# Two operand halves in one buffer: a decoder trunk kernel whose conv and gate projections stream 272, 256 and 272 columns instead of 264, 264 and 264

## What is computed

```python
def _mixer(h, S0, buf0, pos, w_in, w_out, ...):
    z = h @ w_in                                    # 2048 -> 7168 columns
    q, k, v, g_r, a, b, g_c = jnp.split(z, SPLITS, axis=-1)   # 7 x 1024
    ...retention over 8 heads from q, k, v, gated by silu(g_r)...
    u = a * jax.nn.sigmoid(b)                       # conv branch input
    full = jnp.concatenate([buf0, u], axis=1)
    c = depthwise_conv(full, w_dw) + b_dw           # width 31
    c = jax.nn.silu(_layer_norm(c, g_cn, b_cn))
    c = c @ w_pw2 + b_pw2
    conv_out = c * jax.nn.silu(g_c)
    m = jnp.concatenate([ret_out, conv_out], axis=-1) @ w_out
```

## Time and profile before

| | |
|---|---|
| median of 3 runs | 1278.45 us (1275.1 to 1279.62) |
| span of the profiled execution | 1272.7 us |
| PE / PEld busy | 1218.1 us (96%) / 1195.9 us |
| DVE busy | 919.9 us (72%) |
| ACT busy | 613.6 us (48%) |
| POOL busy | 136.4 us (11%) |
| chain that ended last | PE 81%, DVE 9%, issue 4%, ACT 3% |

### The profile page before, as it was taken

How to read it: one execution, slowest core, us unless ns; L and a number is a source line. 1 busy time by engine, 2 the same in 40 slices (tenths; PEclk the granted TensorE clock), 3 DMA queues, 4 the chain that set the end, 5 groups by cost and what they waited for, 6 DMA issues and landing times.

```text
span 1272.7 us, 25528 instructions
## 1 busy us (share of the span) xinstructions
PE 1218.1 (96%) x9814; PEld 1195.9 (94%) x9814; DVE 919.9 (72%) x1404; ACT 613.6 (48%) x952; POOL 136.4 (11%) x188
## 2 busy tenths in 40 slices
PE   5999999999999999889998999999999999997998
PEld 5999899999989999789998999999999999996998
DVE  6798898888976532477868879988889764326673
ACT  6342555555546444635544335555554554455341
POOL 0000011112100012401110000211111000123000
PEclk9999999999999999989999999999999999997999
DMA  7555654454543553515554565555544445533462
GB/s 266 189 211 189 191 198 170 180 198 174 211 148 141 202 194 118 182 69 197 198 196 170 199 204 193 182 194 191 192 167 167 154 176 186 182 117 132 152 224 89
DMA packets 42595, 225.71 MB, mean 177 GB/s; under 512 B 6176, under 2 KB 12320, under 8 KB 18976
## 3 DMA queue, kind: packets, MB, share of 16 engines
q1 hardware_dynamic: 28800, 201.47, 44.6%
q10 hardware_dynamic: 13728, 23.33, 5.5%
HBM read 210.97 MB, written 13.81 MB: 177 GB/s over the span
## 4 chain that ended last, share of the span: by engine, by line
PE 81%; DVE 9%; issue 4%; ACT 3%; POOL 1%; DMA 1%; ACTq 0%; POOLq 0%; DVEq 0%; SPq 0%
PE ps L424 24%; PE ps L425 23%; PE ps L426 23%; DVE wlo L940 3%; PE ps L487 2%; DVE acc L1247 1%; ACT whi L637 1%; PE ps L517 1%; PE ps L518 1%; PE ps L519 1%; DMA raw<-w_in 1%; DVE tmp L1025 1%; POOL acc L1416 1%; DVE c_buf L1025 1%; PE ps L479 0%
## 5 line engine op out<-in xcount | busy, mean ns | idle before, releaser
L424 PE MATMUL ps<-a_hi,whi 128*128 128x264 f32 x2112 | 612.7, 290 | 27.0 <-DVE wlo L940 13.7
L425 PE MATMUL ps<-a_lo,whi 128*128 128x264 f32 x2112 | 600.9, 285 | 0.0
L426 PE MATMUL ps<-a_hi,wlo 128*128 128x264 f32 x2112 | 600.4, 284 | 0.0
L940 DVE TENSOR_TENSOR wlo<-raw,whi 128x2048 fp32r<-128x2048 f32 x192 | 435.5, 2270 | 217.0 <-ACT whi L637 214.8
L424 PEld LDWEIGHTS ps<-a_hi,whi 128*128 128x128 f32 x2112 | 400.0, 189 | 39.0 <-issue 21.8
L637 ACT ACTIVATE whi<-raw 128x2048 fp32r<-128x2048 f32 (+1 forms) x188 | 351.4, 1873 | 150.2 <-DMA raw<-w_in 71.3
L425 PEld LDWEIGHTS ps<-a_lo,whi 128*128 128x128 f32 x2112 | 400.6, 190 | 0.1
L426 PEld LDWEIGHTS ps<-a_hi,wlo 128*128 128x128 f32 x2112 | 398.5, 189 | 0.0
L424 PE MATMUL ps<-b_hi,whi 128*128 128x264 f32 x672 | 191.1, 284 | 1.6 <-ACT tmp L899 1.6
L425 PE MATMUL ps<-b_lo,whi 128*128 128x264 f32 x672 | 190.4, 283 | 0.0
L426 PE MATMUL ps<-b_hi,wlo 128*128 128x264 f32 x672 | 190.3, 283 | 0.0
(11 more groups left out here) (186 smaller groups left out, 1196.3 us busy)
## 6 DMA issues: line engine op xcount, KB each, us to landing
raw<-w_in SPq DMA_DIRECT2D x112, 1024.0 KB, 4.9
raw<-w_out SPq DMA_DIRECT2D x32, 1024.0 KB, 4.8
raw<-w_gate SPq DMA_DIRECT2D x32, 1024.0 KB, 4.8
s_new<-s_ret ACTq DMA_DIRECT2D x16, 512.0 KB, 5.5
ss_out<-s_new ACTq DMA_DIRECT2D x16, 512.0 KB, 2.9
raw<-w_pw SPq DMA_DIRECT2D x8, 1024.0 KB, 4.8
raw<-w_ple SPq DMA_DIRECT2D x8, 512.0 KB, 3.6
x<-x_t SPq DMA_DIRECT2D x4, 528.0 KB, 9.4
```

Source lines behind the costliest of these rows:

```text
L424: pe.matmul(accum[bank][:, 0:R], whi[:, slot, w:w + P], hi, start=k == 0, stop=False)
L425: pe.matmul(accum[bank][:, 0:R], whi[:, slot, w:w + P], lo, start=False, stop=False)
L426: mm = pe.matmul(accum[bank][:, 0:R], wlo[:, slot, w:w + P], hi, start=False, stop=k == k_tiles - 1)
L940: v.tensor_tensor(wlo[:, slot, 0:cols], raw[:, slot % RAW, 0:cols], whi[:, slot, 0:cols].bitcast(F32), ALU.subtract).then_inc(s.lo_ready, 1)
```

## The change

- `a_hi` and `a_lo` become one array `a_ops` with a pitch of 544 floats (2176 bytes) per k: the low half at float 0 (`LO`, 264 floats), the high half at float 264 (`HI`). The last 8 floats of the low half, the samples, now lie directly ahead of the high half. All writers and readers of `a_hi` and `a_lo` use these places.
- In the conv and gate stages (`shared_tail`) the three matmuls of a k are: high weights by 272 columns (8 low samples and 264 high) into PSUM columns 0 to 271; high weights by the 256 low prompt columns into columns 8 to 263; low weights by the same 272 columns. The prompt's sum then stands in columns 8 to 263; the samples' sum is in two parts, columns 0 to 7 and 264 to 271.
- VectorE joins the two parts: in place of one operation of 264 columns that read a tile it does three (`scaled`): a reduce over pairs to 8 columns (`tails`), the scaling of the 256 prompt columns, and the scaling of the 8 joined ones, which waits for the reduce and releases the bank.
- All other products keep 264 columns. `in_a` for them reads `a_ops` at floats 264 and 0 of each k, so that the high half starts 1056 bytes and the low half 0 bytes from the k's start.

The diff, cut to its core:

```diff
+LO, HI, PITCH = 0, R, 544
+TAIL = DEC
+WIDE = R + TAIL
...
-    a_hi = sb("a_hi", [P, KT, R], F32R)
-    a_lo = sb("a_lo", [P, KT, R], F32R)
+    a_ops = sb("a_ops", [P, KT, PITCH], F32R)
...
+    tails = sb("tails", [P, 2, DEC])
...
                 w = at + P * k
+                if operands is shared_tail:
+                    both, low = a_ops[:, k, HI - TAIL:HI + R], a_ops[:, k, LO:LO + SEQ]
+                    pe.matmul(accum[bank][:, 0:WIDE], whi[:, slot, w:w + P], both, start=k == 0, stop=False)
+                    pe.matmul(accum[bank][:, TAIL:TAIL + SEQ], whi[:, slot, w:w + P], low, start=False, stop=False)
+                    mm = pe.matmul(accum[bank][:, 0:WIDE], wlo[:, slot, w:w + P], both, start=False,
+                                   stop=k == k_tiles - 1)
+                    continue
                 hi, lo = operands(k)
...
-        in_a = lambda k: (a_hi[:, k, :], a_lo[:, k, :])
+        in_a = lambda k: (a_ops[:, k, HI:HI + R], a_ops[:, k, LO:LO + R])
...
+        def join_tail(bank, n):
+
+            pair = accum[bank][:, 0:WIDE].rearrange("p (j c) -> p c j", c=TAIL)[:, :, ::WIDE // TAIL - 1]
+            v.tensor_reduce(tails[:, bank, :], pair, AX.X, ALU.add).then_inc(s.tail_joined, 1)
+
+        def scaled(dst, bank, n, by=1.0):
+
+            join_tail(bank, n)
+            v.scalar_tensor_tensor(dst[:, 0:SEQ], accum[bank][:, TAIL:TAIL + SEQ], by, r_x[:, 0:SEQ], ALU.mult, ALU.mult)
+            dve.wait_ge(s.tail_joined, n + 1)
+            v.scalar_tensor_tensor(dst[:, SEQ:R], tails[:, bank, :], by, r_x[:, SEQ:R], ALU.mult,
+                                   ALU.mult).then_inc(acc_free[bank], 1)
...
-            v.tensor_tensor(tmp[0][:, :], accum[0][:, 0:R], r_x[:, :], ALU.mult).then_inc(acc_free[0], 1)
+            scaled(tmp[0], 0, 2 * ct + 3 * CT * l)
...
-            v.scalar_tensor_tensor(tmp[1][:, :], accum[1][:, 0:R], 0.5, r_x[:, :], ALU.mult,
-                                   ALU.mult).then_inc(acc_free[1], 1)
+            scaled(tmp[1], 1, 2 * ct + (3 * CT * l + 1), 0.5)
...
-                v.tensor_tensor(tmp[t % 2][:, :], accum[t % 2][:, 0:R], r_x[:, :],
-                                ALU.mult).then_inc(acc_free[t % 2], 1)
+                scaled(tmp[t % 2], t % 2, 3 * CT * l + 2 * CT + t)
```

24 lines of the change are left out of this document (14 added, 10 removed).

## The result

| | before | after |
|---|---|---|
| median, 20 runs each, side by side | 1276.82 us (1273.15 to 1280.78) | 1280.67 us (1277.76 to 1286.02) |
| ratio | | 1.0038, 95% interval 1.0025 to 1.0050 |
| span of the profiled execution | 1272.7 us | 1279.0 us |

The change makes the kernel 4.9 us slower (3.2 to 6.4, by the means of the runs; the two medians lie 3.9 apart). The forecast was +4.1 us.

What follows compares the result with a forecast made beforehand. TensorE, busy 96% of the span, was taken as the bound. Columns +2.0, conv and gate addresses -1.5, addresses elsewhere +1.8 and VectorE's read +1.8 gave +4.1 on 1278.45: 1282.5 us, range 1275 to 1288.

Steps and rivals of the forecast that it cites:

- case A: Whole kernel: the terms as summed, 1282.5 us (1280.5 to 1284.5), conv tile 5.78 to 5.84 us; chance 0.42.
- D: Heads pay 2.9 ns a k, conv addresses gain nothing, the three-part read costs 0.3 us: +9.4, 1287.9 us; chance 0.16.
- addresses elsewhere: Heads, upper output projection, embedding: halves starting 32 bytes apart cost 1.5 ns on 1248 k, +1.8 us (0 to +3.6).
- join: VectorE's three-part read of conv and gate tiles: 0.15 us more at 12 places on the chain, +1.8 us.
- Columns: Conv and gate matmuls: 800 instead of 792 columns a k, 3.3 ns more on 608 k, +2.0 us.
- Addresses in conv and gate: Conv and gate streams always start where k 0 or k 4 did: 2.5 ns less a k, -1.5 us.
- The rule on lines of 16 bytes: All SBUF streams fill such lines whole, so addresses cost nothing; only columns and VectorE count: +3.8 us, 1282.3.
- The cover that I named for the other reads: Other 36 reads hide behind TensorE's 5.80 us tiles; in the conv loop 1.7 us more fits VectorE's 5.89 left.
- The room of 0.34 us at conv tile 5: Tightest conv read releases at 58.05, tile 7 starts at 58.39; the longer read takes 0.14 us of that.
- an exposed latency for each instruction that reads SBUF: VectorE's read: by this rule two short operations count in full, +3.8 us at the 12 places; forecast kept 0.15 each.
- B: Conv and gate matmuls keep 120.8 ns despite columns and addresses; only VectorE's 1.8 us show: 1280.2 us; chance 0.25.
- C: Conv and gate streams on even addresses and whole 64-byte blocks lose surcharge: 1271.4 or 1275.7 us; chance 0.17.

Runs made afterwards that it cites:

- e6_join: Kernel before, with only VectorE's conv and gate read changed to the three operations (reduce, 256 columns, 8 columns behind a wait): ratio 1.0005 to before.
- e5_widths: Kernel before with streams of 272, 256 and 272 columns in conv loop and gate stage, start addresses and single read kept: 370.4 ns a k, ratio 1.0020.
- e7_hi_only: Changed kernel, but the third matmul of a k streams only the 264 high columns: 367.0 ns a conv k, ratio 1.0034 to the kernel before.
- e2_pitch272: Kernel before with both halves' tiles 272 floats apart instead of 264, equal starts kept: conv k 368.3 / 363.3 ns, ratio 1.0013.
- e9_no_join: Changed kernel, but VectorE reads each tile with one operation of 264 columns, low samples left out: ratio 1.0040 to the kernel before.
- e8_join_more: Kernel before with VectorE's three-operation read plus four more short reduces in every read: ratio 1.0048 to before.
- e1_layout: Changed kernel's buffer layout, but the 264-column streams and single read of before: 364.7 ns a conv k, ratio 1.0025 to the kernel before.
- e3_shift: Kernel before with only the low half's array moved by 32 bytes: 365.3 ns a conv k, ratio 1.0034.
- e11_shift128: Kernel before with only the low half's array moved by 128 bytes: 364.2 ns a conv k, ratio 1.0023.
- e4_wide: Kernel before with 272 columns in all three matmuls of a k in conv loop and gate stage: 379.2 ns a conv k, one run.

## Why the prediction was right, and where it was not

The sum was +4.1 us and the runs gave +4.9, and the median of 1280.67 us lies in the range. Of the signs that the forecast named, the one for case A failed: a conv tile is 5.87 and 5.92 us long, outside 5.78 to 5.84. A head tile is 5.84, between my 5.82 and D's 5.85; the read's 0.49 us came as said, with no wait inside and no new wait of TensorE inside the conv loop. So the total is A's and the way to it is not. The terms behind it:

| term | forecast | measured |
|---|---|---|
| columns and addresses in conv and gate | +0.8 ns a k, +0.5 us | +4.2 (layer 0), +7.5 (layer 1) in conv, about +3.6 us |
| addresses elsewhere | +1.5 ns a k, +1.8 us | +2.4 ns a k, on fewer k, about +2.3 us |
| join | 0.15 us a read at 12 reads, +1.8 us | 0.15 a read, 0.12 to 0.18 at the places looked at; e6_join +0.6 us (-1.4 to +2.8) |
| sum | +4.1 | 6.5 to 7.4 from the terms; runs 4.9 (3.2 to 6.4) |

*Columns.* This is the step that failed. "Eight columns at 0.417 ns are 3.3 ns a k more" took the surcharge of 10.8 ns for fixed. It is not: over the kernels it lies between 10.8 and 13.1 ns in conv. e5_widths, with the addresses of before and the widths of the changed kernel, takes 7.9 ns a k more and not 3.3; on 608 k that is 4.8 us in place of 2.0. e7_hi_only, with eight columns fewer than the changed kernel, is no faster in conv and 2 to 6 ns a k faster in the gate stage.

*Addresses in conv and gate.* I read k 0 and k 4 of one tile as 360 ns and concluded that a kernel which always starts there gains 2.5 ns a k. The reading was right, even conservative (the starts of many tiles put these k at 357 and 358 ns). But a short k is part of a rhythm over eight k whose sum is 2.90 us, in which others take longer, and e2_pitch272, whose starts are k 0's, k 4's and two more, has no such gain in conv, 363.3 and 368.3. No run has the starts of the changed kernel with 264 columns. The nearest comparison is e5_widths, which has the same widths: against its 370.4 the changed kernel takes 366.7 and 370.0 in conv and 370 and 366.5 in the gate stage, 0.4 to 3.9 ns less and 2.1 in the mean. So a gain of the size of my 2.5 may be there at these widths, but it is not one number, and the second product's start in PSUM differs as well. What is shown is the sum of both steps, +0.8 ns a k by the forecast and +4 to +7.5 by the tiles.

*Addresses elsewhere.* The mechanism was right (unequal starts cost), and the row of the pointwise product, 2.9 ns, was nearer to the truth than my half of it: 2.4 in the heads, 2.5 in the upper half of the output projection (ten tiles 58.20 us against 58.00, with half their k on `a_ops`). The number of k was too high. The 12 tiles from head 1 to head 4 of each layer gain or lose nothing as a whole (84.10 and 84.19 us), which the chain's shares did not show. Taking them off leaves 1248 - 288 = 960 k (96 of the 384 were off already), and 960 x 2.4 = 2.3 us.

*The rule on lines of 16 bytes*, by which addresses would be free and the time 1282.3: shifts of 32 and of 128 bytes, both whole such lines, moved a matmul by 0.9 and 0.6 ns and the time by 4.3 and 2.9 us. The specifications in the Trainium skill ("SBUF — State Buffer") are no guide to this cost.

*Join.* The group is 0.49 us long and waits nowhere inside, both as forecast. The count of reads was a little high: the earlier trace rows has five full pieces in a layer, and the sixth, at 116.59, is 0.06 us long, which leaves ten places and 1.5 us. Between the kernel before and the changed one the join is hard to see. TensorE's waits behind reads in layer 0 went from 0.99, 1.29 and 1.16 us to 1.14, 1.23 and 1.20 at the first three places, so the full 0.15 shows at one of three. That one, in order of time on PE, before and after:

```profile
32.09 0.39 PE L424 MATMUL ps<-a_hi,whi 128*128 128x264 f32 x1 [0.99 <-DVE tmp L986]
```

```profile
32.45 0.39 PE L433 MATMUL ps<-a_ops,whi 128*128 128x272 f32 x1 [1.14 <-DVE tmp L1009]
```

The comparison with e9_no_join has the same streams on both sides, and there the waits differ by the whole join at all of these places. The tiles ahead of them are slower after the change, which shortens the same waits; that is the likely reason why it shows at one of three here. So the runs of e6_join, read alone, say 0.6 us, and the waits and e8_join_more speak for more, up to the 1.5 us of ten places. That the join was priced too high is not shown.

The cover that I named for the other reads, the slack of VectorE in the conv loop, is real: of the 4.36 us that e6_join leaves, e8_join_more uses up 2.0, and conv tiles 8 to 16 still run at TensorE's pace. The room of 0.34 us at conv tile 5 is borne out too: in e8_join_more, where the read releases about 0.43 us later, tile 7 takes 0.11 us more (5.91 for 5.80). The statement that the Trainium skill ("VectorE: DVE Perf Modes", the TRN2 errata) makes on an exposed latency for each instruction that reads SBUF would, as I used it, have priced a short operation at its full 0.15 to 0.17 us. The trace doesn't bear that out: the scaling of the 8 joined columns, which reads SBUF, is followed after 0.08 us (52.77 to 52.85, above).

*Sum.* The terms by the trace add up to 6.5 us with the join at 0.6 and to 7.4 with it at 1.5, both above the interval. For e1_layout the same count (608 x 2.2 + 960 x 2.4 ns = 3.6 us) meets 3.2, for e3_shift (608 x 2.8 + 960 x 2.9 = 4.5) 4.3, for e11_shift128 (608 x 1.7 + 960 x 2.1 = 3.1) 2.9, for e5_widths (its loop and gate tiles, 544 k on the path x 7.9 = 4.3) 2.6 with an interval that reaches 4.5. So only for the changed kernel is the count clearly too high. The stretches that can be read directly give 4.4 us; the count has 2.1 to 3.0 us more in the stretches with waits, and the runs leave 0.5 for them (-1.2 to +2.0). That slower matmuls shorten a wait there, as in the heads 1 to 4, would explain it. Another possible reason is that the slower pace does not come everywhere in every execution, as the gate stage of layer 0 shows; with 366.7 throughout, the terms for conv and gate are 2.6 us in place of 3.6. How much each takes stays open.

*The rivals.* B (TensorE does not notice) is out by the tile times. C (even starts and whole blocks are cheap) is out by the changed kernel's own tiles, which have both, and so are its halves, even starts by e2_pitch272 and whole blocks by e4_wide. D had the full price in the heads and no gain in conv, and was nearer than A in both (2.4 ns against 2.9 and 1.5; +4.2 and +7.5 ns a k against 3.3 and 0.8); it failed in the join at 0.3 us. The forecast came out near the truth by luck: the term for conv and gate was 3.1 us too small, and what made up for it is that the runs show less than the terms add up to, for which the forecast had no step.

## What to carry to other kernels

When TensorE runs back to back, take its pace from starts some hundred matmuls apart and compare it between layouts; a mean over a full repetition is a price, a single short interval inside it is a weak hint at one. Before a run is taken as the price of one part of a change, check that its streams start where those of the changed kernel do. Moving an operand array by 32 bytes cost 4.3 us here, about as much as the whole change, so a change of layout is to be timed alone, first, with everything else left as it was. Work added to another engine is free up to a point; add it in larger doses to find the point, as the single dose is lost in the noise of the runs, and compare the waits of two kernels that differ in nothing but that work, for a wait also shrinks when the work ahead of it gets slower.
